# A two-layer trunk step: down products of the expert passes put off by one pass, first loads and decays moved into the projections

## What is computed

```python
for l in range(2):
    m = adaln(cond, w_mod[l], b_mod[l])              # 6 sections (shift, scale, gate), from SiLU(cond)
    h = modulate(y, m[0], m[1])
    if l == 0: o = retention(h) ++ neighbourhood_attention(h)   # w_in 1024x3072, decays, cached keys/values
    else:      o = gated_short_conv(h) ++ attention(h)          # w_in 1024x2560
    y = post_norm(y, o @ w_out, m[2])
    h = modulate(y, m[3], m[4])
    score = sigmoid(h @ router_w)                    # 64 experts, 8 taken per token
    for each expert e:                               # gate and up: 1024x128, down: 128x1024
        out[its tokens] += weight * (silu(h @ w_gate[e]) * (h @ w_up[e])) @ w_down[e]
    y = post_norm(y, out + shared_expert(h), m[5])
```

## Time and profile before

| what | value |
|---|---|
| runs | 1192.82, 1197.23, 1196.08 us; median 1196.08 |
| profiled execution | 1196.54 us |
| its span on the core | 1194.4 us |
| TensorE matmuls busy | 1083.5 us (91%) |
| VectorE, ACT, GpSimd busy | 537.7, 403.0, 51.7 us |
| chain that ended last | TensorE 86%, VectorE 6%, DMA 4%, ACT 2% |
| moved by DMA | 303.24 MB, 254 GB/s over the span |

### The profile page before, as it was taken

One profiled execution on the slowest core, in us unless ns is written; L12 is line 12 of the kernel. 1 busy time (PEld: TensorE's weight loads), 2 busy tenths in 40 slices (PEclk: granted clock), 3 DMA queues, 4 the chain that ended last, 5 costly groups with the idle time before them and its releaser, 6 DMA issues.

```text
span 1194.4 us, 30538 instructions
## 1 busy us (share of the span) xinstructions
PE 1083.5 (91%) x12866; PEld 711.9 (60%) x12866; DVE 537.7 (45%) x1122; ACT 403.0 (34%) x764; POOL 51.7 (4%) x85
## 2 busy tenths in 40 slices
PE   3699897899999999999985987789999999999993
PEld 1589786555555555555544987665555555555541
DVE  1433665444434444334337484545443443444435
ACT  3433323233333333223225453323333333333331
POOL 2100010000000000110000101000000000000000
PEclk9799997999999999999996988799999999999997
DMA  9995855599999997554416743529999999600000
GB/s 330 354 333 191 309 206 212 190 394 409 408 408 408 408 407 283 181 218 171 144 37 211 190 168 117 212 103 391 408 408 408 408 408 408 268 2 2 2 2 36
DMA packets 106079, 303.24 MB, mean 254 GB/s; under 512 B 9132, under 2 KB 40012, under 8 KB 105944
## 3 DMA queue, kind: packets, MB, share of 16 engines
q1 hardware_dynamic: 94176, 262.17, 57.4%
q0 software_dynamic: 10576, 37.20, 9.0%
q10 hardware_dynamic: 1192, 1.92, 0.4%
HBM read 500.06 MB, written 2.52 MB: 421 GB/s over the span
## 4 chain that ended last, share of the span: by engine, by line
PE 86%; DVE 6%; DMA 4%; ACT 2%; issue 1%; SPq 1%; DVEq 0%; ACTq 0%
PE ps L1544 83%; DMA slab<-in_w_mod 4%; PE ps L1547 4%; DVE temp L1202 1%; DVE small L1204 1%; DVE temp L1201 1%; DVE slab L1057 0%; ACT temp L886 0%; ACT hi_main L761 0%; SPq L605 0%; SPq L517 0%; DVE slab L1313 0%; DVE x_tok L1228 0%; ACT slab L892 0%; DVE temp L1226 0%
## 5 line engine op out<-in xcount | busy, mean ns | idle before, releaser
L1544 PE MATMUL ps<-slab 128*32 128x256 f32 (+2 forms) x7792 | 544.8, 423 | 3.3 <-DVE slab L1313 2.0
L1544 PEld LDWEIGHTS ps<-slab 128*32 128x32 f32 (+1 forms) x7792 | 262.2, 111 | 268.2 <-issue 148.1
L1406 DVE SCALAR_TENSOR_TENSOR o_lo<-ps,ex,o_hi 128x512 fp32r<-128x512 f32 x192 | 143.9, 751 | 176.3 <-ACT o_hi L930 171.6
L930 ACT ACTIVATE o_hi<-ps,ex 128x512 fp32r<-128x512 f32 x192 | 132.2, 688 | 209.5 <-PE ps L1544 198.8
L920 ACT ACTIVATE slab<-ps 128x128 f32<-128x128 f32 x96 | 26.6, 277 | 269.5 <-PE ps L1544 269.5
L1389 DVE TENSOR_TENSOR ex<-slab,ps 128x128 f32<-128x128 f32 x96 | 27.5, 287 | 190.3 <-ACT slab L920 190.3
L1544 PE MATMUL ps<-pick_at,x_hi 128*128 128x256 f32 x384 | 106.9, 311 | 0.7 <-ACT slab L892 0.4
L1013 DVE TENSOR_TENSOR lo_main<-slab,hi_main 128x2048 fp32r<-128x2048 f32 x30 | 68.7, 2291 | 81.0 <-ACT hi_main L761 77.0
L1544 PEld LDWEIGHTS ps<-pick_at,x_hi 128*128 128x128 f32 x384 | 72.0, 188 | 39.6 <-issue 36.7
L1544 PE MATMUL ps<-pick_at,x_lo 128*128 128x256 f32 x384 | 95.6, 281 | 0.0
L1313 DVE COPY slab<-ps 128x512 f32<-128x512 f32 x96 | 66.4, 692 | 61.6 <-PE ps L1544 61.6
(11 more groups left out here) (234 smaller groups left out, 1015.4 us busy)
## 6 DMA issues: line engine op xcount, KB each, us to landing
slab<-in_exp_w_gate SPq DMA_DIRECT2D x256, 512.0 KB
slab<-in_exp_w_up SPq DMA_DIRECT2D x256, 512.0 KB
slab<-in_exp_w_down SPq DMA_DIRECT2D x256, 512.0 KB
slab<-in_w_mod SPq DMA_DIRECT2D x24, 1024.0 KB, 10.1
slab<-in_w_in_even SPq DMA_DIRECT2D x12, 1024.0 KB, 8.2
slab<-in_w_in_odd SPq DMA_DIRECT2D x10, 1024.0 KB, 6.0
temp<-in_w_mod POOLq DMA_DIRECT2D x8, 1024.0 KB, 5.8
slab<-in_w_mod POOLq DMA_DIRECT2D x8, 1024.0 KB, 6.5
```

Of the source, the lines that this page charges most:

```text
L930: nc.scalar.activation(o_hi[:, c * 512:(c + 1) * 512], ps[:, 6 + c, :], ACT.Copy, scale=slot_gate[:, j % 2:j % 2 + 1]).then_inc(o_hi_out, 1)
L1406: V.scalar_tensor_tensor(out=o_lo[:, cols], in0=ps[:, 6 + c, :], scalar=slot_gate[:, j % 2:j % 2 + 1], in1=o_hi[:, cols].bitcast(F32), op0 ...
L1544: return nc.tensor.matmul(out, w, x, start=start, stop=stop)
```

## The change

In the expert stage the order of a pass on TensorE becomes up(j), turned(j - 1), gather(j), scatter(j - 2), over_jobs or next_mods (j - 1), down(j - 1), over 49 rounds; ACT's and VectorE's loops follow, with `norm_tokens` and `over_jobs` of pass j (`extras`) in round j + 1. The wait of the up products on `over_out` is kept as it was. SP loads gate and up of pass j + 1 ahead of down of pass j. At the start only the first 139 columns of the constants are loaded ahead of x; logits, `early` (now in `next_third`) and the other 800 columns go out on ACT's queue behind the split of unit 1, and the caches, states and bias rows of GpSimd's queue after unit 0. The turning of x stands after mod 3, that of the cached keys after unit 1. The decays are computed in two steps: ACT's behind the copies of units 1 and 2, VectorE's at units 2 and 4.

```diff
-KEPT = dict(ident=128, cos=64, sin=64, window=128, one=1, ln_eps=1, rms_eps=1, fold=4 * 2,
+KEPT = dict(ident=128, one=1, ln_eps=1, rms_eps=1, fold=4 * 2, cos=64, sin=64, window=128,
...
+FIRST_N = KEPT_AT["cos"][0]
...
-        early = part(PROJ_AT, EARLY_N)
+        early = next_third[:, :, :].rearrange("p a n -> p (a n)")[:, 0:EARLY_N]
...
+                load_up(l, 0)
                 for j in range(ARRAYS):
-                    load_array(l, j)
+                    if j + 1 < ARRAYS:
+                        load_up(l, j + 1)
+                    load_down(l, j)
...
-            pool.wait_ge(main_used, len(FIRST_MODS) - MOD_RAW)
+            pool.wait_ge(main_used, len(FIRST_MODS) + 1)
...
             act.dma_start(bias_rows, A["b_mod"].rearrange("l (s n) -> (l s) n", s=6)).then_inc(mod_bias_in, 16)
-            act.dma_start(early, A["shape_consts"][:, KEPT_N:EARLY_END]).then_inc(early_in, 16)
...
+            def late_loads():
...
+                act.dma_start(early, A["shape_consts"][:, KEPT_N:EARLY_END]).then_inc(early_in, 16)
+                act.dma_start(const[:, FIRST_N:], A["shape_consts"][:, FIRST_N:KEPT_N]).then_inc(rest_in, 16)
...
+            def decays(step):
+                if step == 0:
+                    act.wait_ge(decay_in, 48)
+                    act.wait_ge(consts_in, 16)
...
+                else:
+                    act.wait_ge(decay_ready, 2)
+                    act.wait_ge(early_in, 16)
...
                 if l == 0 and n == 0:
-                    act.wait_ge(k_dec_ready, 1)
...
                 make_x(l, 0, 0, 1)
-                if l == 0:
...
                 for n in range(IN_UNITS[l]):
                     split_to(in_unit(l, n + 1) if n + 1 < IN_UNITS[l] else out_unit(l, 0))
+                    if l + n == 0:
+                        late_loads()
                     unit_copy(l, n)
+                    if l == 0 and n in (1, 2):
+                        decays(n - 1)
+                    if l == 0 and n == 2:
+                        act.wait_ge(cache_t, 1)
+                        nc.scalar.activation(kc_t, ps[:, 7, :].rearrange("p (h t) -> p h t", h=H), ACT.Copy) \
+                            .then_inc(cache_t_out, 1)
...
+            def decays(step):
...
+                if step == 0:
+                    dve.wait_ge(decay_ready, 1)
...
+                else:
+                    dve.wait_ge(decay_ready, 16)
...
+                    V.memset(small[:, 48:49], 0.0).then_inc(k_dec_ready, 1)
+                    dve.wait_ge(rest_in, 16)
...
+            def extras(l, j, bank):
+
+                if j < 2:
+                    norm_tokens(l, 0, j)
+                if j < 3:
+                    over_jobs(l, j, bank)
+                if l + 1 < DEPTH and next_group(j) is not None:
+                    next_rows(j, bank)
+                if l + 1 < DEPTH and j in NEXT_FOLD:
+                    next_section_out(j, bank)
...
+                    if j < ARRAYS:
+                        dve.wait_ge(silu_out, last + 1)
+                        V.tensor_tensor(slot_h, slot_silu, ps[:, slot_bank(j), HID:2 * HID], ALU.mult).then_inc(h_ready, 1)
+                    if j > 0:
+                        dve.wait_ge(slot_t_out, 2 * last)
+                        V.tensor_scalar(put_at[:, (j - 1) % 2, :], turned_pick, 0.0, None, ALU.not_equal)
+                        V.tensor_reduce(slot_gate[:, (j - 1) % 2:(j - 1) % 2 + 1], turned_pick, AX.X, ALU.max).then_inc(put_out, 1)
                     if block + 1 < BLOCKS:
                         slots_from(l, block + 1, 2 * a + 1)
-                    dve.wait_ge(slot_t_out, 2 * done)
-                    V.tensor_scalar(put_at[:, j % 2, :], turned_pick, 0.0, None, ALU.not_equal)
-                    V.tensor_reduce(slot_gate[:, j % 2:j % 2 + 1], turned_pick, AX.X, ALU.max).then_inc(put_out, 1)
-                    if j < 2:
-                        norm_tokens(l, 0, j)
...
-                    for c in range(2):
-                        dve.wait_ge(o_hi_out, 2 * (done - 1) + c + 1)
-                        cols = slice(c * 512, (c + 1) * 512)
...
+                    if a == 0 and block < BLOCKS:
+                        pick_gates(l, block)
+                    if j > 0:
+                        extras(l, j - 1, slot_bank(j - 1))
+                        for c in range(2):
+                            dve.wait_ge(o_hi_out, 2 * (last - 1) + c + 1)
+                            cols = slice(c * 512, (c + 1) * 512)
...
                         norm_tokens(l - 1, 1, n)
+                    if l == 0 and n in (2, 4):
+                        decays(n // 2 - 1)
...
+            def up_products(l, j):
...
+                if 2 <= j < 5:
+                    pe.wait_ge(over_out, 3 * l + j - 1)
...
+                for k in range(KC):
+                    for t in range(4):
+                        ins = mm(ps[COL * t:COL * (t + 1), bank, 0:2 * HID], x_slots[:, block % 2, k, a, COL * t:COL * (t + 1)],
+                                 ring(slots[t])[:, 0:2, k * HID:(k + 1) * HID], k == 0, k == KC - 1)
+                ins.then_inc(slots_mm, 1)
...
+            def slots_turned(l, j):
+
+                block, a, bank = j // BLOCK, j % BLOCK, slot_bank(j)
+                pe.wait_ge(h_ready, l * ARRAYS + j + 1)
+                pe.wait_ge(gates_ready, l * BLOCKS + block + 1)
+                turned(ps[:, bank, TOK:TOK + P], slot_h)
+                turned(ps[:, bank, TOK + P:TOK + 2 * P], pick_gate[:, a]).then_inc(slot_t, 1)
+
+            def gather_next(l, j):
+
+                block, a = j // BLOCK, j % BLOCK
+                pe.wait_ge(picks_ready, l * BLOCKS + block + 2)
...
+                        pe.wait_ge(slots_out[i], (l * BLOCKS + 1) * KC // 2 + 1)
...
+            def down_products(l, j):
...
+                pe.wait_ge(slot_t_out, 2 * (now + 1))
+                if j < 3:
+                    over_jobs(l, j, bank)
+                if l + 1 < DEPTH and j >= NEXT_FROM:
+                    next_mods(j, bank)
+                for slot, use in RING_SLOTS[j]:
+                    pe.wait_ge(ring_down[slot], loads_of(l, slot, use))
+                block, a = (j + 1) // BLOCK, (j + 1) % BLOCK
+                for i in range(2):
+                    if j + 1 < ARRAYS - BLOCK:
+                        pe.wait_ge(slots_out[i], (l * BLOCKS + block + 1) * KC // 2 + a + 1)
+                    else:
+                        pe.wait_ge(o_lo_out, 2 * (now - 1) + i + 1)
+                    for t in range(4):
+                        ins = mm(ps[COL * t:COL * (t + 1), 6 + i, :], slot_ht[:, COL * t:COL * (t + 1)],
...
+                for j in range(ARRAYS + 1):
+                    if j < ARRAYS:
+                        up_products(l, j)
                     if j > 0:
-                        scatter(l, j - 1)
-                    pe.wait_ge(slot_t_out, 2 * (now + 1))
-                    if j < 3:
-                        over_jobs(l, j, bank)
-                    if l + 1 < DEPTH and j >= NEXT_FROM:
-                        next_mods(j, bank)
-                    for slot, use in RING_SLOTS[j]:
-                        pe.wait_ge(ring_down[slot], loads_of(l, slot, use))
-                    for i in range(2):
-                        if block + 1 < BLOCKS:
-                            pe.wait_ge(slots_out[i], (l * BLOCKS + block + 1) * KC // 2 + a + 1)
-                        else:
-                            pe.wait_ge(o_lo_out, 2 * (now - 1) + i + 1)
-                        for t in range(4):
-                            ins = mm(ps[COL * t:COL * (t + 1), 6 + i, :], slot_ht[:, COL * t:COL * (t + 1)],
-                                     ring(slots[t])[:, 2, i * 512:(i + 1) * 512], True, True)
-                        ins.then_inc(down_mm, 1)
+                        slots_turned(l, j - 1)
+                    if j < ARRAYS - BLOCK:
+                        gather_next(l, j)
+                    if j > 1:
+                        scatter(l, j - 2)
+                    if j > 0:
+                        down_products(l, j - 1)
                 scatter(l, ARRAYS - 1)
...
-                    mods(FIRST_MODS[:5])
-                    section_fold(0)
-                    mods(FIRST_MODS[5:7])
+                    mods(FIRST_MODS[:4])
                 x_turned(l, 0)
                 if l == 0:
-                    mods(FIRST_MODS[7:])
-
-                    pe.wait_ge(cache_k_in, 16)
-                    for h in range(H):
-                        ins = turned(head(7, h), kc_in[:, h])
-                    ins.then_inc(cache_t, 1)
+                    section_fold(0)
+                    mods(FIRST_MODS[4:])
                     section_fold(1)
...
-                    if l == 0 and n == 0:
+                    if l == 0 and n == 1:
+                        pe.wait_ge(cache_k_in, 16)
+                        for h in range(H):
+                            ins = turned(head(7, h), kc_in[:, h])
+                        ins.then_inc(cache_t, 1)
```

(56 more changed lines are left out.)

174 lines of the change are left out of this document (64 added, 110 removed).

## The result

| what | value |
|---|---|
| runs of the changed kernel | 1229.80, 1229.83, 1232.33, 1314.92 us; median of the first three 1229.83 |
| kernel before, 4 runs | median 1196.65 us |
| ratio to before | 1.0285, 95% interval 1.0253 to 1.0317 |
| profiled execution's span | 1227.6 us (before 1194.4) |
| TensorE matmuls busy | 1090.2 us, 89% |

Forecast were 1196.4 us and a range of 1189 to 1204, so 1229.8 is outside. The chain already says something new: SP's queue has 8% of it, where it had 1%.

The account below looks back on a forecast made before the run. The prediction took TensorE's own time to bound the expert passes and loads to bound the start. Start -3.65 and two layers' passes +4.0 gave +0.35 on a median of 1196.08, so 1196.4 us, range 1189 to 1204.

Parts of the forecast that it names:

- The middle: Expert passes away from a layer's ends: same TensorE instructions in another order, so a pass stays at 7.80 us.
- (c): Kept wait on `over_out`: up products of passes 2 and 3 wait 2.4 and 1.5 us; +3.9 us a layer, bounds 2 to 5.
- the clock falls in the new waits: Rival, 8%: up products of passes 2 and 3 run slower after idle TensorE, +3 us each; 1202 or 1208 us.
- The three terms of TensorE's side: In the `over_out` wait: transposes and gathers 1.4, counts' matmuls 0.6, down products 1.75 us, summed there as 3.85.
- the cached keys: Start: their transposes between units cost 0.65 us plus a load wait near 0.2, up to 3.5; together +1.15 us.
- (a): Last four passes of each layer: TensorE's four waits for VectorE's h go, -3.1 us; pass 0's wait, -0.5.
- (b): Last round of each layer: no up products to hide o_lo, so +1.5 us idle ahead of the scatter.
- The start: Everything up to the routing: first unit -5.7, cached keys +1.15, decays +0.9, together -3.65 us.
- the loss at unit 4: Start: the decays' second step and the keys' copy make ACT's and VectorE's split late; +0.9 us (0 to 3).
- The dearer round: Rival, 9%: tile shape changes make every expert pass dearer by 0.08 us or more; 1203 to 1205 us.
- the cheaper one: Rival, 15%: every expert pass 0.08 us cheaper, together with a first unit at its -7.5 bound; 1188 to 1190 us.
- the chance of slower: Whole kernel slower by over 0.5%, above 1202.1 us: 0.17, from the slow order's 9% and the clock's 8%.

Follow-up runs that it names:

- e2: Changed kernel with VectorE's wait for the picks in a block's first round asking for one transpose less; 1211.34 us, ratio 1.0119.
- e1: Changed kernel with SP reading an overflow pass's four job numbers once and keeping them for the down loads; 1218.28 us, ratio 1.0181.
- e5: Kernel before with only SP's four job numbers of an overflow pass read a second time ahead of the down weights; 1210.90 us, ratio 1.0117.
- e8: e4 with SP's old order of loads put back (gate, up, down of a pass, then the next pass; numbers kept); 1403.32 us, ratio 1.1718.
- e3: Changed kernel with VectorE's counts of the overflow jobs ahead of the two products over x_tok; 1220.37 us, ratio 1.0204.
- e4: Changed kernel with three edits together: job numbers read once, picks waiting for one transpose less, counts ahead of x_tok; 1184.04 us, ratio 0.9902.
- e9: e4 with both decay steps put off: ACT's behind the copies of units 3 and 4, VectorE's at units 4 and 6; 1185.79 us, ratio 0.9906.

## Why the prediction was wrong, point by point

**The middle: the step that failed.** "In the middle the same instructions stand in another order: 7.80 stays. Its loads keep their distance, three passes from release to use." Of TensorE's own instructions this was nearly right: 7.75, so the claim that an order without waits cannot shorten 7.80 was off by 0.05, some 4 us over 88 rounds. It looked at TensorE only, and it failed in two places.

- *The picks.* VectorE's wait at a block's start is nowhere in the sum. I had counted what stands behind moved instructions for `over_out`, but not for `slot_t`, whose count in `picks` stayed the same while the transposes moved one round. 0.85 us idle and 1.12 us of round, ten rounds a layer: 18.5 us by e2.
- *SP.* `load_down` reads the job numbers a second time, and SP's instructions stand at nothing in the sum, with no reason given. The 144 GB/s of the earlier trace rows are of a window that begins in the primary passes; in the overflow passes of layer 1 it is 2 GB/s. A quiet DMA says nothing of its issuer's time: SP spends it on reading numbers and on issues even if they move nothing. 11.6 us by e1 and 14.0 by e5. The three passes of distance hold for the primary passes alone; e8 shows what it means that they don't hold for four slots of six. The change had taken care of this by its order of loads, and the forecast gave it no price.

**(c), the wait on `over_out`: mechanism and size right, the clock missing.** Forecast 2.4 and 1.5 us in front of the up products of passes 2 and 3, released by L1383 and L1391; measured 2.34 and 1.20 by just these lines. The rival "the clock falls in the new waits" held 8% and was partly true: behind the wait of 2.34 us 1.69 us more in five of six cases (two layers each of the changed kernel, e1 and e2), nothing behind 1.20. It had +3 for each. The whole term was 10.9 us in e3's passes, forecast 7.8. The three terms of TensorE's side, 1.4 + 0.6 + 1.75, are 3.75 and not 3.85, and the longest wait for the cached keys by its own row is 3.75 and not 3.5; neither matters.

**(a), (b).** The four waits for h are gone. The rounds without gathers take 6.80 in e4 (forecast 6.82). In the end drain the last two scatters wait 1.22 and 1.59 us, where only the second stood before: 1.2 us more idle time, forecast +1.5.

```profile
1203.70 0.49 PE L1587 MATMUL ps<-o_hi,put_at 64*128 64x512 f32 x2 [1.22 <-DVE o_lo L1463]
1208.34 0.50 PE L1587 MATMUL ps<-o_hi,put_at 64*128 64x512 f32 x2 [1.59 <-DVE o_lo L1463]
```

e4_all_three, which has none of the three losses, closes the sum: its passes take 8.3 us less than before. The forecast without its term (c) is 3.8 less, and 0.05 us in each of 88 rounds another 4.4.

**The start: right.** From the changed kernel's timeline:

```profile
40.76 2.04 PE L1587 MATMUL ps<-x_hi,hi_main 128*128 128x256 f32 x8 [3.09 <-ACT x_hi L842]
48.51 1.07 PE L1587 MATMUL ps<-slab,cond_pad 128*32 128x256 f32 x16
55.36 0.60 PE L1590 MATMUL ps<-const,temp 128*128 128x128 f32 x4
70.50 1.07 PE L1587 MATMUL ps<-slab,cond_pad 128*32 128x256 f32 x16 [0.64 <-DMA slab<-in_w_mod]
125.52 2.05 PE L1587 MATMUL ps<-slab 64*128 64x128 f32 x16 [0.69 <-ACT slab L877]
```

The first unit starts 5.3 us earlier, mod 8 is at 48.51 ("near 48"), and the first projection ends 3.87 us earlier, where -3.65 was forecast (3.5 between the means of all profiles with either start). The parts were less exact, and part of the close agreement is luck: the cached keys cost 0.44, not 1.15 (in e4 their wait was there, 0.55, and they cost 1.20), and the loss at unit 4 came as a wait for mod 11 and not for ACT's split. Its mechanism stays open after e9.

**The rivals.** The dearer round did not come true, the cheaper one by more than half, 0.05 of its 0.08 us, and the losses hide it. That the chance of slower was 0.17 rests on the missing SP and VectorE terms: each alone would have left the range.

## What to carry to other kernels

When a stage is put off by one step, list every wait on every engine that counts that stage, and ask of each whether its number should move too: two of three losses here were waits whose number stayed. An engine that issues loads has a pace of its own; price its register reads and issues per pass, above all where the loads move nothing. And let the order of loads in one queue follow the order in which their slots come free; where it didn't, the loader and the computing engine took turns (e8).

## What the runs showed that I had not expected

- Four register reads a pass on SP, 2.7 us between an up and a down issue, are worth 14 us in 12 or so passes with 2 GB/s of traffic.
- An idle time of 2.34 us in front of the up products was followed by a lower clock in five cases of six and by none in the sixth, with the same instructions ahead of it. In e1's two layers that is the difference of 5.35 and 3.66 us. At the late mod of the attention stage 2.62 us idle were followed by half clock (kernel before), and 1.21 to 1.42 us by full clock in the other eleven profiles.
- Putting off the down products without the new order of loads costs 219 us; with it and the three mends the same idea is 10 us faster than before. e4_all_three, at 0.990 of the kernel before, beats both kernels.
